# Second attention block of a fused transformer kernel: 21 weight tiles as three one-pass products of float32r halves, gate halves spread among merges, norm squares chunk by chunk

## The chip, the cores and the metric

One core of a Trainium2 chip runs the whole program in one launch. The metric is the device time of one execution, in microseconds. Engines are named as in the profile: PE (TensorE), DVE (VectorE), ACT (ScalarE), POOL (GpSimd), SP (SyncE, which issues most DMAs here).

## The reference, cut to what matters

Two blocks are computed one after the other on a sequence of 512 tokens of width 1024. The first (a gated delta rule beside a forgetting attention, then a SwiGLU feed-forward network, FFN) ends in a norm. The second begins so:

```python
h = modulate(rmsnorm_2(x, norm1_g), shift1, scale1)
q, k, v, cb, cc, cu = split(h @ w_in)             # 512, 128, 128, 512, 512, 512 columns
q, k = rope(rmsnorm_2(q, q_norm_g)), rope(rmsnorm_2(k, k_norm_g))
attn = sliding_window_attention(q, k, v, sinks)   # window 128, 8 query heads, 2 key heads
conv = cb * short_conv(cc * cu, conv_w)           # 3 taps
merged = concatenate([rmsnorm_2(attn), rmsnorm_2(conv)])
x = x + gate1 * (merged @ w_out)
h2 = modulate(rmsnorm_2(x, norm2_g), shift2, scale2)
x = x + gate2 * peer(h2, ...)                     # top-k experts: most of the time, not touched
```

All of it is float32. A result has to agree with a float32 computation.

## The kernel before, in words

Activations lie transposed, 128 features on the partitions and 512 tokens along the row, eight such chunks for 1024 features. A weight tile is 1024 x 128, eight chunks of 128 x 128; one product of it with the activations fills one PSUM bank.

**Order.** Each engine runs its own list of instructions in the order written, and semaphores connect the lists. Nothing is reordered by a planner: an instruction that waits holds up all that stands behind it on its engine.

**The first block.** After the delta rule's preparation a loop goes through `schedule()`: merges of triangular inverses (`merge_p`, `merge_y`; POOL makes their masked operands at L740) alternate with steps of the forgetting attention (`attend_scores`, `attend_turn`, `attend_out`). `gate_half(k, j)` (L1118) is half of a weight tile for the output gate, four tiles in all: tiles 0 and 1 are done inside the preparation, both halves of tile 2 right before the loop, and those of tile 3 after the loop's second `merge_p` and its second `attend_scores`.

**The FFN.** 68 weight tiles (`ITEMS_F`) are each split into a float32r high part by ACT (`split_high`, L1693) and a low part by DVE (`split_low`, L2204), three tiles ahead of PE, and multiplied in three passes (`split_product`, L1201 to L1203: high x high, high x low, low x high). The last eight tiles are the last third of the down projection. Each is added to the residual by DVE (`residual`, L2198).

**The norm between the blocks.** ACT squares each of the eight residual chunks twice (L1749, L1750), once scaled, for two norms. POOL adds the squares up chunk by chunk (`add_square`, L753), and PE turns the sums into means (`mean_sum` L1175, `mean_last` L1180). ACT takes roots (L1731), DVE reciprocals, and DVE and ACT write the modulated input `u2` in halves of 256 tokens (L2326, L1741).

**The second block's input projection.** `first_pair` (L1265) multiplies the first two q tiles while `u2` is still being written. Then 15 tiles go through `product` (L1244), plain float32: q2, q3, k (`for f in range(2, 5)`), and cc0, cu0 to cc3, cu3 and cb0 to cb3 (`conv_products`). For q and k, ACT copies each tile out (L1760), squares it (L1766) and takes the root of a mean (L1756), DVE does a reciprocal (L2363), scales and rotates (L2357 to L2359), and PE makes the mean and the turn (L1250, L1256). DVE uses that loop for the last norm of the residual too: two chunks for each tile (`last_norm`, L2334).

**The window loop.** Eight steps s (four blocks of 128 queries by two key heads). PE: a conv product, four or eight transposes (L1352), scores of the next step (L1333), in steps 1, 3 and 5 a second conv product, then the output (L1367). DVE: mask (L2401), maximum (L2403), in between a part of the convolution (`conv_step`), the copy of the step before (`window_out`, L2378), then the division (L2413). ACT: exponentials (L1797, L1799), copies of the transposes (L1806).

**Behind it.** Norms of both halves of `mix`, `half_mix` (L1385) for the first two output tiles, `product` for the other six, the residual (L2424).

**Transfers.** SP issues them in order, each `fill` after a wait for the reader of what lay in its slot before. Two slots of 16 KB a partition take turns. In the second block SP's list is: F_Q2, F_KV2, two fills F_CU2 (cc and cu), F_CB2 (cb), then a wait for `pool_step` 10 and four DMAs that write zeros to `dense_gates` in HBM (L612, 25.2 MB), then F_OUT2 and F_OUT2 + 1 (output tiles 0 to 3 and 4 to 7), then the next stage's weights. `pool_step` 10 is POOL's memset of the source row (L775), which waits for all eight `last_norm` chunks (`x2_ready`):

```python
pool.wait_ge(S["x2_ready"], DC)
step(pool.memset(zeros, 0.0))
```

Of the kernel before, what the change touches and what calls it, by code (L numbers as in the profile page):

```python
# [21 lines left out]
P = 128  # L22
# [43 lines left out]
CUT, SPLIT_FLOATS = 12675, 22656  # L66
# [53 lines left out]
def program(nc, io):  # L120
    places, n_const = const_places()
    ctx = ExitStack()
    with ctx:
# [11 lines left out]
        with nc.sbuf_tensor("split", [P, SPLIT_FLOATS], F32R) as split:  # L135
            pass
# [134 lines left out]
        keep = top[0]  # L271
        qkr = carve(5, SEC)
        vt2 = carve(SC, P)
        prod = carve(2, SEC + CK2 - 1)
        cc = carve(2, SEC)
        y2 = carve(CW // P, SEC)
        mix = carve(DC, SEC)
        sq2 = carve(2, SEC)
        tm2 = carve(2, SEC)
        ex = carve(PER, 2 * P)  # L280
        pT2 = carve(2, PER * P)
        mxs, nms, rss, ess = (carve(PER) for _ in range(4))
        top[0] = max(top[0], ffn_end)
        cosT, sinT, angT = (carve(SEC) for _ in range(3))
        assert top[0] <= over_rstd - MOD_W
# [30 lines left out]
        gate_of = carve(SEC)  # L316
        zeros = carve(DEN)
# [76 lines left out]

        def chunks_of(i):
# [55 lines left out]
        def tile_out(p):  # L451
# [6 lines left out]
            first = 5 if f == 15 else 0  # L458
# [23 lines left out]
        def _(sp):  # L482
# [126 lines left out]
            fill(F_CB2, halves(F_CB2, w2[:, :, c_cb:c_cb + 512]), "p2_ready", 5 + SC + 2)  # L609
# [5 lines left out]
            for k in range(2):  # L615
                fill(F_OUT2 + k, halves(F_OUT2 + k, wo2[:, :, k * 512:(k + 1) * 512]), "p2_ready", 5 + SC + 4 * (k + 1))
            wq = io["wq"].rearrange("(c p) n -> p c n", p=P)
            for k in range(4):
                reader, count = ("out2_done", 4 * (k + 1)) if k < 2 else ("wq_done", 4 * (k - 1) + 2)
# [210 lines left out]
        def _(pe):  # L830
# [222 lines left out]
            def attend_scores(s):  # L1053
# [4 lines left out]
                else:  # L1058
                    pe.wait_ge(S["proj_taken"], 29)
# [13 lines left out]
            def attend_turn(s):  # L1073

# [33 lines left out]
            def gate_half(k, j):  # L1108
# [6 lines left out]
                elif k == 0:  # L1115
                    pe.wait_ge(S["proj_taken"], FIRST + 1)
                for c in range(DC):
# [14 lines left out]
            for j in range(2):  # L1132
                gate_half(2, j)

            for what, a, s in schedule():
# [1527 lines left out]
```

## Time and profile before

| | us |
|---|---|
| median of three runs | 2430.11 |
| lowest and highest | 2428.63, 2436.08 |
| the profiled execution | 2433.65 |
| its span, first to last instruction | 2431.8 |
| PE's share of the chain that ended last | 95% |

The span is read in stages: projections and merges up to about 490 us, the output projection and the FFN from 490 to 882, the norm to 896, the input projection to 953, the window loop to 1066, the output projection to 1130, query scoring to 1264, and the experts to the end. A row of the timeline gives the start and the duration in us, the engine, the line, out<-in with partitions x elements, and in brackets how long the engine had stood idle and who released it. Matmuls overlap, so that the distance from one start to the next, not the duration, is what one costs.

### The profile page before, as it was taken

To read this page: it belongs to the slowest core of one execution; us is meant where nothing else is said; L and a number is where in the kernel's file an instruction comes from. 1 tells how busy PE (TensorE), PEld (TensorE's weight loads), DVE (VectorE), ACT (ScalarE), POOL (GpSimd) and SP (SyncE) were. 2 spreads that over 40 slices of the span, in tenths; PEclk is the share of its full clock that TensorE was granted. 3 is DMA by queue.
4 is the path that set the end of the run, shared out by engine and by line. 5 is a ranking of instruction groups with operands and counts; after the bars stand their busy time and mean duration, and the time that the engine had idled before them with its cause. 6 is when DMAs were issued, how large, how long until landed. Compare 5 with 4: busy or idle time off the path is not lost.

```text
span 2431.8 us, 33626 instructions
## 1 busy us (share of the span) xinstructions
PE 2394.3 (98%) x11435; PEld 1467.0 (60%) x11435; DVE 1437.0 (59%) x2831; ACT 874.3 (36%) x1385; POOL 1063.3 (44%) x739
## 2 busy tenths in 40 slices
PE   8999999999999989999999999999999999999999
PEld 6888677658888865445554444444444466666665
DVE  4412455456868547444949894222222399989998
ACT  3222223232232242223135555445445433333332
POOL 0001111010000020001788888888888175578886
PEclk9999889999999999999999999999999999999999
DMA  7240100165666312852436666666666799999997
GB/s 206 70 72 1 53 10 10 70 178 162 189 180 196 87 52 70 322 196 87 87 44 149 150 156 151 148 155 154 147 153 155 251 397 382 370 359 374 367 370 286
DMA packets 437700, 426.49 MB, mean 175 GB/s; under 512 B 104808, under 2 KB 359912, under 8 KB 437488
## 3 DMA queue, kind: packets, MB, share of 16 engines
q1 hardware_dynamic: 353456, 332.85, 43.0%
q0 software_dynamic: 84160, 92.58, 15.4%
q8 instruction: 46, 0.75, 0.1%
q14 instruction: 38, 0.31, 0.0%
HBM read 364.28 MB, written 61.05 MB: 175 GB/s over the span
## 4 chain that ended last, share of the span: by engine, by line
PE 95%; DVE 2%; ACT 1%; issue 1%; SPq 0%; POOL 0%; DMA 0%; DVEq 0%; ACTq 0%; POOLq 0%
PE psum L1469 9%; PE psum L1471 9%; PE psum L1470 9%; PE psum L1492 7%; PE psum L1494 7%; PE psum L1493 7%; PE psum L1244 6%; PE psum L889 6%; PE psum L1201 5%; PE psum L1203 5%; PE psum L1202 5%; PE psum L1450 4%; PE psum L1104 1%; PE psum L1081 1%; PE psum L969 1%; PE psum L1062 1%
## 5 line engine op out<-in xcount | busy, mean ns | idle before, releaser
L786 POOL DMA_INDIRECT dense_gates<-arena x384 | 607.2, 1581 | 151.6 <-issue 116.7
L1469 PE MATMUL psum<-arena 128*128 128x512 bf16 x1024 | 389.8, 381 | 0.0
L1471 PE MATMUL psum<-arena 128*128 128x512 bf16 x1024 | 387.6, 379 | 0.0
L1470 PE MATMUL psum<-arena 128*128 128x512 bf16 x1024 | 386.9, 378 | 0.0
L2535 DVE TENSOR_TENSOR arena<-arena,psum 128x1024 bf16<-128x1024 f32 x124 | 151.5, 1222 | 352.1 <-ACT psum L1845 351.5
L1494 PE MATMUL psum<-arena,low 128*128 128x384 bf16 x1024 | 334.3, 326 | 0.0
L1492 PE MATMUL psum<-arena,low 128*128 128x384 bf16 x1024 | 334.3, 326 | 0.0
L1493 PE MATMUL psum<-arena,low 128*128 128x384 bf16 x1024 | 334.3, 326 | 0.0
L1861 ACT ACTIVATE low<-low 128x1024 bf16<-128x1024 f32 x128 | 135.3, 1057 | 294.2 <-PE psum L1494 272.0
L814 POOL DMA_INDIRECT arena<-gelu_spill,arena x128 | 184.8, 1444 | 87.3 <-DMA gelu_spill<-cst 43.3
L806 POOL DMA_INDIRECT arena<-in_v,arena x128 | 178.9, 1398 | 84.0 <-DVE arena L2582 55.9
L1201 PE MATMUL psum<-split 128*128 128x512 f32 x528 | 207.2, 392 | 0.6 <-DVE low L2198 0.6
L1203 PE MATMUL psum<-split 128*128 128x512 f32 x528 | 205.8, 390 | 0.0
L1202 PE MATMUL psum<-split 128*128 128x512 f32 x528 | 205.7, 390 | 0.0
L1851 ACT ACTIVATE cst<-psum 128x512 f32<-128x512 f32 x128 | 76.6, 598 | 307.6 <-PE psum L1471 307.5
L2569 DVE TENSOR_TENSOR low<-low 128x1024 bf16<-128x1024 f32 x128 | 156.9, 1225 | 34.1 <-ACT low L1861 34.1
L1470 PEld LDWEIGHTS psum<-arena 128*128 128x128 bf16 x1024 | 101.2, 99 | 121.4
L1469 PEld LDWEIGHTS psum<-arena 128*128 128x128 bf16 x1024 | 99.6, 97 | 121.3
L1471 PEld LDWEIGHTS psum<-arena 128*128 128x128 bf16 x1024 | 98.9, 97 | 122.6
L2582 DVE SCALAR_TENSOR_TENSOR arena<-arena 128x1024 f32<-128x1024 f32 x127 | 163.2, 1285 | 11.2 <-DMA arena<-in_v,arena 1.2
L753 POOL TENSOR_TENSOR arena<-arena 128x512 f32<-128x512 f32 x25 | 31.6, 1281 | 290.1 <-ACT arena L1784 108.9
L759 POOL DMA_DIRECT2D arena<-in_ada_w x12 | 10.9, 908 | 323.2 <-DVE arena L2231 243.5
(377 smaller groups left out, 3945.2 us busy)
## 6 DMA issues: line engine op xcount, KB each, us to landing
arena<-in_uT SPq DMA_DIRECT2D x128, 512.0 KB, 4.6
low<-in_v SPq DMA_DIRECT2D x128, 512.0 KB, 5.5
gelu_spill<-cst SPq DMA_DIRECT2D x128, 256.0 KB, 3.4
arena<-in_ada_w POOLq DMA_DIRECT2D x12, 2048.0 KB, 9.2
dense_gates<-arena SPq DMA_DIRECT2D x4, 6144.0 KB, 40.0
arena<-gelu_spill SPq DMA_DIRECT2D x128, 192.0 KB, 5.8
arena<-dense_gates SPq DMA_DIRECT2D x128, 192.0 KB, 7.0
low<-in_w_in SPq DMA_DIRECT2D x20, 1024.0 KB, 7.4
```

The source lines that it names most:

```text
L786: pool.indirect_dma_start(gate_cells, bass.IndirectOffsetOnAxis(ap=cell_of[:, n:n + 1], axis=0), gate_of[:, n:n + 1], None, compute_op=ALU ...
L806: pool.indirect_dma_start(vrow[n % ROWS], None, table, bass.IndirectOffsetOnAxis(ap=slot_row[:, n:n + 1], axis=0)).then_inc(S[f"row_in{n % ...
L814: pool.indirect_dma_start(slot_act[:, n:n + 1], None, cells, bass.IndirectOffsetOnAxis(ap=slot_cell[:, n:n + 1], axis=0)).then_inc(S[f"cel ...
L1201: mm(out, wh[:, c, :], hi[:, c, :], start=c == 0, stop=False)
L1202: mm(out, wh[:, c, :], lo[:, c, :], start=False, stop=False)
L1203: last = mm(out, wl[:, c, :], hi[:, c, :], start=False, stop=c == n - 1)
L1469: mm(psum[:, bank, :], hi[:, c, :], h2hi[:, c, :], start=c == 0, stop=False)
L1470: mm(psum[:, bank, :], hi[:, c, :], h2lo[:, c, :], start=False, stop=False)
L1471: last = mm(psum[:, bank, :], lo[:, c, :], h2hi[:, c, :], start=False, stop=c == DC - 1)
L1492: mm(psum[:, f, 0:DEN], vh[:, cols], wh, start=start, stop=False)
L1493: mm(psum[:, f, 0:DEN], vh[:, cols], wl, start=False, stop=False)
L1494: last = mm(psum[:, f, 0:DEN], vl[:, cols], wh, start=False, stop=stop)
```

## The change

21 tiles of the second block (q2, q3, k, all of cc, cu and cb, and output tiles 2 to 7) are split as the FFN's are and multiplied in three passes by a new `product_2`. They go in the order of `ITEMS_2`, through the FFN's three pairs of buffers. ACT writes the high part (`split_high_2`) and DVE the low part (`split_low_2`). The activations `u2`, and later `mix`, get a high and a low part too (`bhi`, `blo`). In the window loop the splits of step s stand in `SPLIT_AT[s]`. The slots' fills now wait for the low parts (`fw_lo`). `last_norm` moves from the q and k loop into the window loop's first four steps. The order of SP's list and the wait for `pool_step` 10 in it stay as they were.

Apart from that, the second half of gate tile 2 moves behind the loop's first `attend_scores`, and the second half of tile 3 behind the first `attend_turn`; and ACT squares each residual chunk when it is ready, among the last FFN tiles, instead of behind them. Tiles are placed anew in the memory to make room.

```diff
+        ITEMS_2 = [("q", 2), ("q", 3), ("k", 0)]
+        ITEMS_2 += [(what, j) for j in range(4) for what in ("cc", "cu")] + [("cb", j) for j in range(4)]
+        ITEMS_2 += [("o", f) for f in range(2, DC)]
+        SPLIT_AT = [(6, 7), (8,), (9, 10), (11,), (12, 13), (14,), (15, 16), (17,)]
...
@@ SP
+                sp.wait_ge(S["fw_lo"], F_ALL + 2 + k)
                 fill(F_CU2 + k, ...
-                     "p2_ready", 4 if k == 0 else 5 + SC)
-            fill(F_CB2, halves(...), "p2_ready", 5 + SC + 2)
+                     "p2_ready", 2 if k == 0 else 5 + SC)
+            fill(F_CB2, halves(...), "fw_lo", F_ALL + place_2["cc", 2])
             sp.wait_ge(S["pool_step"], 10)
             for q in range(4):
                 sp.dma_start(io["dense"]...)
...
-                fill(F_OUT2 + k, halves(...), "p2_ready", 5 + SC + 4 * (k + 1))
+                fill(F_OUT2 + k, halves(...), "fw_lo", F_ALL + place_2[("cb", 0) if k == 0 else ("o", 2)])
...
@@ PE
+            def product_2(bank, i, sig, between=None):
+                pe.wait_ge(S["fw_lo"], F_ALL + i + 1)
+                wh, wl = fwh[i % SPLITS], fwl[i % SPLITS]
                 for c in range(DC):
                     if between and c == 4:
                         between()
+                    mm(psum[:, bank, :], wh[:, c, :], bhi[:, c, :], start=c == 0, stop=False)
+                    mm(psum[:, bank, :], wh[:, c, :], blo[:, c, :], start=False, stop=False)
+                    last = mm(psum[:, bank, :], wl[:, c, :], bhi[:, c, :], start=False, stop=c == DC - 1)
+                last.then_inc(S[sig], 1)
...
-            for j in range(2):
-                gate_half(2, j)
+            gate_half(2, 0)
...
                     attend_scores(s)
-                    if s == 1:
-                        gate_half(3, 1)
+                    if s == 0:
+                        gate_half(2, 1)
...
                         attend_turn(s - 2)
+                    if s == 2:
+                        gate_half(3, 1)
...
@@ ACT
+                if what == "down" and q == 2 and k:
+                    norm_squares(k - 1)
...
+            def split_high_2(i):
+                if i < SPLITS:
+                    act.wait_ge(S["ffn_ps"], F_ALL)
+                else:
+                    sig, count = done_2(i - SPLITS)
+                    act.wait_ge(S[sig], count)
+                n, w = raw_2(i)
+                if i == 0 or raw_2(i - 1)[0] != n:
+                    act.wait_ge(*fill_done(n))
+                f_(fwh[i % SPLITS], w, ACT.Copy).then_inc(S["fw_hi"], 1)
+            for c in range(DC):
+                act.wait_ge(S["shifted"], c + 1)
+                f_(bhi[:, c, :], u2[:, c, :], ACT.Copy).then_inc(S["h2_hi"], 1)
+                if c >= DC - SPLITS:
+                    split_high_2(c - (DC - SPLITS))
...
@@ ACT, window loop
                 ins.then_inc(S["a_tc"], 1)
+                for i in SPLIT_AT[s]:
+                    split_high_2(i)
                 if s == 1:
                     take_c(1)
                 elif s == 6:
                     conv_square(0)
                     conv_square(1)
...
@@ DVE
-                if j < 4:
-                    last_norm(2 * j)
-                    last_norm(2 * j + 1)
+                if j >= 2:
+                    split_low_2(j + 1)
...
@@ DVE, window loop
                     conv_step(s - 1)
                     window_out(s - 1)
+                    for i in SPLIT_AT[s - 1]:
+                        split_low_2(i)
+                if s < 4:
+                    last_norm(2 * s)
+                    last_norm(2 * s + 1)
                 dve.wait_ge(S["a_e"], s + 1)
...
+            for k, c in enumerate((4, 5, 6, 7, 0, 1, 2, 3)):
+                dve.wait_ge(S["h2_hi"], DC + k + 1)
+                dve.tensor_tensor(blo[:, c, :], mix[:, c, :], bhi[:, c, :], ALU.subtract).then_inc(S["h2_split"], 1)
```

## Rows read from the trace of the kernel before

**Rows 1.** Windows: length, busy PE PEld DVE ACT POOL (count), clock, DMA share, GB/s.
```profile
953.00:1066.00 113.00, 112.16 (x328) 53.10 (x327) 49.35 (x91) 29.47 (x96) 1.27 (x1) 1.00 0.74 268
...
1004.00:1008.00 4.00, 4.00 (x10) 1.76 (x10) 3.86 (x7) 1.08 (x5) 0.00 (x0) 1.00 1.06 401
```
**Rows 2.** Groups by line: count, busy us, mean ns, idle before; the page's part 5.
```profile
L1244 PE MATMUL psum<-arena,low 128*128 128x512 f32 x336 | 148.1, 596 | 0.5 <-DVE arena L2342 0.5
L1201 PE MATMUL psum<-split 128*128 128x512 f32 x528 | 207.2, 392 | 0.6 <-DVE low L2198 0.6
```
**Rows 3.** Timeline of PE in the FFN, 57 matmuls in a row.
```profile
699.62 0.39 PE L1201 MATMUL psum<-split 128*128 128x512 f32 x1
...
712.31 0.39 PE L1203 MATMUL psum<-split 128*128 128x512 f32 x1
```
**Rows 4.** Timeline of ACT and DVE in the FFN: splits of one tile and one chunk.
```profile
701.86 1.06 ACT L1693 ACTIVATE split<-low 128x1024 fp32r<-128x1024 f32 x1 [3.30 <-PE psum L1203]
...
708.69 1.22 DVE L2204 TENSOR_TENSOR split<-low,split 128x1024 fp32r<-128x1024 f32 x1
708.81 0.64 ACT L1716 ACTIVATE split<-low 128x512 fp32r<-128x512 f32 x1 [0.44 <-DVE low L2290]
```
**Rows 5.** Timeline from the end of the FFN to the second block's first product.
```profile
873.69 14.88 POOL L753 TENSOR_TENSOR arena<-arena 128x512 f32<-128x512 f32 x12 [101.60 <-ACT arena L1749]
...
881.80 0.69 DVE L2198 TENSOR_TENSOR low<-low,psum 128x512 f32<-128x512 f32 x1 [3.39 <-PE psum L1203]
...
887.40 3.78 PE L1175 MATMUL psum<-arena,cst 128*128 128x512 f32 x4 [5.70 <-POOL arena L753]
...
892.31 0.69 ACT L1731 ACTIVATE arena<-psum,low 128x512 f32<-128x512 f32 x1 [8.54 <-PE psum L1180]
...
896.06 14.05 PE L1265 MATMUL psum<-arena,low 128*128 128x256 f32 x64 [2.93 <-ACT arena L1741]
...
900.36 3.31 ACT L1741 ACTIVATE arena<-arena,low 128x256 f32<-128x256 f32 x8 [1.66 <-DVE arena L2326]
```
**Rows 6.** Windows of 4 us, columns as in Rows 1: after an idle PE.
```profile
886.00:890.00 4.00, 2.60 (x3) 1.13 (x4) 0.00 (x0) 0.00 (x0) 2.57 (x3) 0.50 0.00 0
```
**Rows 7.** Groups by line, 896 to 953 us: the reciprocals of q and k.
```profile
L2363 DVE RECIPROCAL arena<-arena 128x512 f32<-128x512 f32 x5 | 16.8, 3352 | 9.9 <-ACT arena L1756 9.9
```
**Rows 8.** Timeline of step 4 of the window loop: mask, last exponential.
```profile
1003.93 1.23 DVE L2401 TENSOR_TENSOR arena<-psum,cst 128x1024 f32<-128x1024 f32 x1 [1.55 <-PE psum L1333]
...
1008.90 0.19 ACT L1799 ACTIVATE arena<-arena 128x4 f32<-128x4 f32 x1
```
**Rows 9.** Timeline of POOL's memset and SP's queue; then landing of all fills (L499).
```profile
944.13 0.42 POOL L775 MEMSET arena<- 128x384 f32 x1 [55.56 <-DVE low L2334]
...
981.46 50.05 SPq L612 DMA_DIRECT2D dense_gates<-arena  x4
1031.56 31.43 SPq L499 DMA_DIRECT2D low<-in_w_out  x4
...
DMA to landing us min/median/max: 4.9/7.4/28.5
```
**Rows 10.** Timeline of PE, the last step's transposes.
```profile
1061.88 1.04 PE L1352 MATMUL psum<-cst,arena 128*128 128x128 f32 x8
```
**Rows 11.** Timeline of PE among the merges: two gate halves, the fourth merge.
```profile
248.01 7.39 PE L1118 MATMUL psum<-arena,low 128*128 128x264 f32 x32
...
270.30 1.11 PE L971 MATMUL psum<-cst,low 128*128 128x128 f32 x4
```
**Rows 12.** Timeline of PE, four merges of eight matmuls each.
```profile
294.11 1.16 PE L969 MATMUL psum<-arena,low 128*128 128x128 f32 x8
...
300.75 1.16 PE L969 MATMUL psum<-arena,low 128*128 128x128 f32 x8
...
310.76 1.65 PE L969 MATMUL psum<-arena,low 128*128 128x128 f32 x8
...
321.40 2.08 PE L969 MATMUL psum<-arena,low 128*128 128x128 f32 x8
```

More of the change, by code:

```diff
@@ L135, in program @@
         with nc.sbuf_tensor("split", [P, SPLIT_FLOATS], F32R) as split:
+            pass
+        with nc.sbuf_tensor("below", [P, BELOW_2], F32), nc.sbuf_tensor("split_2", [P, 2 * DC * SEC], F32R) as split_2:
             pass
@@ L271, in program @@
         keep = top[0]
+        sq2 = carve(2, SEC)
+        tm2 = carve(2, SEC)
+        pT2 = carve(2, PER * P)
+        assert top[0] == CUT + BELOW_2
+        bhi, blo = (split_2[:, k * DC * SEC:(k + 1) * DC * SEC].rearrange("p (c t) -> p c t", c=DC) for k in range(2))
+        top[0] += 2 * DC * SEC
+        mxs, nms, rss, ess = (carve(PER) for _ in range(4))
+        assert top[0] <= ffn_end - 2 * SPLITS * DC * P
+        top[0] = ffn_end
+        cosT, sinT, angT = (carve(SEC) for _ in range(3))
+        assert top[0] <= over_rstd - MOD_W
+        vt2 = angT.rearrange("p (a b) -> p a b", a=SC)
+        ex = carve(PER, 2 * P)
+        mix = carve(DC, SEC)
+        y2 = carve(CW // P, SEC)
+        over_zeros = arena_floats - (DC * SEC + P + SEC + DEN)
+        assert top[0] <= over_zeros
+        top[0] = over_zeros + DEN
         qkr = carve(5, SEC)
-        vt2 = carve(SC, P)
         prod = carve(2, SEC + CK2 - 1)
         cc = carve(2, SEC)
[L276 to L285, printed above, removed]
         top[0] = over_rstd + 2 * TP
@@ L1393, in _ @@
             for f in range(2, DC):
-                if f == 4:
-                    pe.wait_ge(*fill_done(F_OUT2 + 1))
+                if f == 2:
+                    pe.wait_ge(S["h2_split"], 2 * DC)
                 pe.wait_ge(S["res2_done"], f - 1)
-                product(f % 2, slot_cols(F_OUT2 + f // 4), slice(f % 4 * P, (f % 4 + 1) * P), mix, "out2_done")
+                product_2(f % 2, place_2["o", f], "out2_done")
             mean_sum(u2, 4 * SUMS + 1)
@@ L1666, in _ @@
                     take(ORDER.index(12 + m // 2))
-            take(ORDER.index(14))
             for what, a, s in schedule():
@@ L1722, in _ @@
                     split_high(ahead)
-            def squares2(ready):
-                for c in range(DC):
-                    act.wait_ge(S[ready], c + 1)
-                    f_(u2[:, c, :], xT2[:, c, :], ACT.Square).then_inc(S["sq_ready"], 1)
+                if what == "down" and q == 2 and k:
+                    norm_squares(k - 1)
             def std2(ready, bank, row, bias):
@@ L1742, in shift @@
                            ).then_inc(S["shifted" if j else "half_shifted"], 1)
-            f_(rstd[:, 1, 0:1], eps[:, 0:1], ACT.Sqrt)
-            act.wait_ge(S["col_sq"], 2)
-            act.wait_ge(S["mod_acc"], MODS * P // MOD_W + 1)
-            for c in range(DC):
-                act.wait_ge(S["res_done"], 3 * DC + c + 1)
-                f_(u2[:, c, :], xT2[:, c, :], ACT.Square, scale=col_sq[:, c:c + 1]).then_inc(S["sq_ready"], 1)
-                f_(sq1[:, c, :], xT2[:, c, :], ACT.Square).then_inc(S["sq1_ready"], 1)
+            norm_squares(DC - 1)
             std2(3, 6, 0, eps_sq)
@@ L1822, in _ @@
                     mix_root(3 - c)
-            act.wait_ge(S["m_done"], DC)
-            squares2("res2_done")
+            for c in (4, 5, 6, 7, 0, 1, 2, 3):
+                act.wait_ge(S["m_done"], (c + 4) % DC + 1)
+                f_(bhi[:, c, :], mix[:, c, :], ACT.Copy).then_inc(S["h2_hi"], 1)
+            for c in range(DC):
+                act.wait_ge(S["res2_done"], c + 1)
+                f_(u2[:, c, :], xT2[:, c, :], ACT.Square).then_inc(S["sq_ready"], 1)
+                if 2 <= c < 5:
+                    split_high_2(place_2["o", c + 3])
             std2(5, 6, 0, eps)
@@ L2329, in _, with split_low_2 @@
             modulated(0, col_n1, DC)
+            def split_low_2(i):
+                dve.wait_ge(S["fw_hi"], F_ALL + i + 1)
+                dve.tensor_tensor(fwl[i % SPLITS], raw_2(i)[1], fwh[i % SPLITS], ALU.subtract).then_inc(S["fw_lo"], 1)
+            for c in range(DC):
+                dve.wait_ge(S["h2_hi"], c + 1)
+                dve.tensor_tensor(blo[:, c, :], u2[:, c, :], bhi[:, c, :], ALU.subtract).then_inc(S["h2_split"], 1)
+                if c >= DC - SPLITS:
+                    split_low_2(c - (DC - SPLITS))
             dve.wait_ge(S["std_ready"], 5)
@@ L2416, in _ @@
             window_out(SC * KV - 1)
+            for i in SPLIT_AT[SC * KV - 1]:
+                split_low_2(i)
             for g in (1, 0):
```

75 lines of the change are left out of this document (48 added, 27 removed).

## The prediction

> **What bounds the kernel now.** The chain of work that ended last lies on PE for 95%. That tells which engine is late on average, not what an edit is worth, so I went through the stages that the change touches and asked in each which wait ends last. In the window loop PE is busy for 112.16 of 113 us [rows 1] and idles 0.5 us ahead of all its products [rows 2]: PE bounds it, and DVE and ACT have more than half of the time free. Behind the FFN, by the timeline, PE stands and waits for POOL's sums. And in the timeline of SP's queue 25.2 MB of zeros are written during the window loop; nobody waits for them now (their rows are named where they are priced). That queue is what I think decides this change, so keep it in mind while PE's gain is worked out.
>
> **PE's gain for one tile.** Two records stand for one float32 matmul: 336 of them take 148.1 us, 0.441 us each with the start of every product in it, some 0.429 inside one; the 16 of a tile are 6.87 us [rows 2]. In the FFN 57 one-pass matmuls start within 12.69 us, one per 0.2266 us [rows 3], so 24 of them take 5.44 us. One tile saves 1.43 us, 21 tiles 30 us, if PE is what each of them waits for.
>
> The Trainium skill (FP8 and Floating Point Precision, TensorE Precision Notes) says that true float32 takes four passes through the array. By that rule three passes save a quarter, 1.72 us per tile; the rows show less, since a split pass costs 0.2266 us and a quarter of a float32 matmul 0.2145. For the six tiles that reach the end in my sum the rule would give 10.3 us, the rows 8.6, which I take.
>
> **The splits.** A tile costs ACT 1.06 and DVE 1.22 us, a chunk of activations 0.64 on ACT [rows 4] and 0.69 on DVE, as another DVE pass of 512 columns [rows 5]. That is 22 and 26 us for the tiles, 10 and 11 us for twice eight chunks.
>
> **Norm squares: 7.9 us earlier.** Now POOL starts at 873.69 and needs 14.88 us for twelve adds, 1.24 each; PE waits 5.70 us for them and starts at 887.40 [rows 5]. With squares made as each residual comes (one per 18 x 0.2266 = 4.08 us) the two adds of a chunk, 2.5 us, are done before the next; those of chunk 6, whose residual starts at 881.80 - 4.08 = 877.7, end near 881.6. The last chunk goes to PE directly: residual until 882.5, square 883.2, mean 884.3. The root moves from 892.31 [rows 5] to 884.4, and the gap in which the clock fell to 0.50, the 1.2 GHz level [rows 6], closes. ACT has 1.3 us more for each tile of 4.08, POOL's adds can delay a low part by one add; three tiles of lead cover both.
>
> **Input projection: 8.2 us earlier.** The first pair, 896.06 to 910.1 [rows 5], goes from 888.2 to 902.2. ACT's list now has eight chunk copies (0.57 each back to back) and three splits ahead of its first copy of a q tile; behind the shifts, which end at 903.7 [rows 5] less 7.9, that lasts until 903.4. The first mean, which waits for copy and square, comes at 904.8, not 902.2. DVE ends its low parts at 905.3, does the reciprocal of the second norm (3.35, as [rows 7]) and only at 908.8 the first of q. From there each tile costs DVE a reciprocal of 3.35 [rows 7], one pass to scale, three to rotate and a split: 7.3 us, against PE's 5.44 and two matmuls of 0.86. PE no longer bounds it; it stalls 1.0 us at the first turn, 0.4 at the last, 1.6 before the first scores. Those come at 945.1 instead of 953.2: of 7.9 + 4 x 1.43 us the stage keeps 8.2.
>
> **The window loop, up to step 3.** A wide step needs 5.2 us from the mask to the last exponential [rows 8]; DVE's own part (two passes of 1.23 and three tiny ones) is 2.95, half as wide (steps 0 and 1) 1.9. Behind it DVE now does, by the widths, a part of the convolution (2.1), `window_out` (0.7), one or two splits (1.23 each), two `last_norm` chunks (1.4) and the division (1.6, narrow 1.1). Step 1: 1.9 + 2.1 + 0.7 + 2.45 + 1.4 + 1.1 = 9.7 us, while PE has one output and one product, 6.5: the transposes come at 963.1 and PE has stood 3.5 us. Step 2, behind a second product and `gated`: 3.0 + 2.1 + 0.7 + 1.2 + 1.4 + 1.6 = 10 us against 5.44; transposes at 982.5, 4.4 us lost. In step 3 the last two `last_norm` chunks end at **993.0**. This is the point that counts. Before, they ended at 944.1, and POOL's memset followed [rows 9], in time for a queue that came to its wait at 981.
>
> **The transfer wall.** SP's order is unchanged: zeros behind `pool_step` 10, F_OUT2 behind the zeros. Before, the zeros were issued from 981.46, and issuing them held SP for 50.05 us; F_OUT2 was issued at 1031.56 and landed 28.5 us later, at 1060.1, though the median fill needs 7.4: it lay behind the zeros [rows 9]. (28.5 is the largest landing of that line; I take it for this fill, the only one issued behind zeros.) Nobody minded, as its first reader, `half_mix`, stands behind step 7. From 981.46 to 1060.1 went 29.4 MB (2.1 of F_CB2, issued just before, 25.2 of zeros, 2.1 of F_OUT2), 374 GB/s. Now the memset ends at 993.5 and the zeros start near 993.8; F_CB2 landed long before; 27.3 MB at 374 GB/s are 73 us, with 1.5 us to start: F_OUT2 lands at **1068.3**. But its reader has moved forward: `split_high_2(15)` in ACT's step 6, which PE's work alone would let run near 1042. Behind that wait on ACT are split 16, two squares, and all exponentials of step 7; DVE needs both high parts before it divides step 7; PE needs DVE. PE ends its last conv product near 1049 and stands for 26 us. From the landing on: two splits 2.1, two squares 1.2, exponentials 2.2, division 1.6, with waits 7.35 us: the transposes of step 7 start at 1075.6, before at 1061.88 [rows 10]. Here the change is 13.8 us behind, and all that PE saved since step 3 is gone.
>
> **Behind the wall.** After 5.7 idle us PE worked at a clock of 0.50 [rows 5, 6]; after 26 it will too: transposes, conv mean and part of the last output at half rate cost 2.2 us (0 if the clock stays). The eight low parts of `mix`, 5.5 us, end 0.4 us later than the first residual lets PE go on. Then six tiles gain 8.6 us. Sum: 13.8 + 2.2 + 0.4 - 8.6 = 7.8 us slower. SP's next weights, for the query stage, start no later than now.
>
> **Gate halves: 1 us more, and the clock.** A half is 3.6 us of PE [rows 11]. The loop's first merge starts that much earlier, but `merge_p` 2 now finds its operand not ready (POOL makes it from DVE's merge 0, which stands behind the scores of step 1): PE idles some 2.7 us where a half had covered it, and the half comes later, ahead of the scores of step 3. By this order the fourth merge moves from 270.30 [rows 11] to 271.2. Bounds: 3.6 us won if a half goes wholly into idle time, 2.7 lost. Worth more is the clock: in this loop eight matmuls that take 1.16 us at times take 2.08, and then two merges with two attention steps between them are 10.64 us apart instead of 6.64 [rows 12]. 16 us in that state cost 6. Moving PE's work by some us can take such an episode away or add one; the trace doesn't say which.
>
> **The sum.** 2433.65 of the profiled execution (span 2431.8 and 1.85 around it) plus 7.8 plus 1.0 is 2442.4. That execution is 3.5 us above the median of the runs; against the median it is 2430.1 + 8.8 = **2439 us**.
>
> **Rivals.**
> *The zeros don't hold F_OUT2 up* (0.16). Then step 7's transposes follow PE's and DVE's own work at 1050.4, 11.5 us earlier than before; one more split ahead of the last squares costs 0.8: 11.5 - 0.8 - 0.4 + 8.6 - 1.0 = 17.9 us won, 2412. Against it stands the landing of 28.5 us. The Trainium skill (DMA: Bandwidth & Descriptors, Issuing engines are not separate DMA queues) says that DMAs from SP, ACT and POOL run on the same engines and interleave; if a fill interleaved so with zeros of its own queue, this rival would be right, and no row here shows that.
> *Full gain* (0.04): DVE keeps up everywhere, 30 + 7.9 us: 2392. DVE's sums above speak against it.
> *Faster zeros* (0.13): at 400 GB/s, as around 1004 [rows 1], F_OUT2 lands 4.7 us earlier: 2434.
> *A clock episode less* (0.18): 2433. *One more* (0.13): 2445. This is the slower side's own mechanism: it decides where PE's idle pieces before 271 us fall close together.
> *The forecast* (0.36): 2439, own range 2433 to 2444.
>
> **Chances and range.** A measurement of this kernel can tell 0.3%, 7.3 us: from 2422.8 to 2437.4 is no change. Faster: 0.16 + 0.04, and 0.04 from two favourable cases together: 0.24. Same: the rest of these two cases and the forecast's low end: 0.33. Slower: 0.43. The range 2412 to 2448 leaves out the full gain, half of the first rival and the bad cases added up, 0.16.
>
> **What would show it.** In the profile after: product matmuls 0.227 us apart; the root behind the FFN at 884.4; the memset at 993 and zeros issued right behind it; a hole of 20 to 30 us in PE between 1049 and 1076, where ACT's first split of an output tile waits for a DMA; a clock of 0.50 behind it; DVE's reciprocals of q and k nearly back to back. Without the hole the first rival is right. If the memset comes before 980, my chain of DVE in steps 1 to 3 is too long; if the hole is there and the time still under 2423, the wall is right and its neighbours are mis-sized.

## The result and the profile after

The changed kernel takes 2447.66 us (median of 20 runs, 2436.09 to 2452.09) against 2432.01 us for the kernel before, taken beside it (20 runs): a ratio of 1.0066 with a 95% interval of 1.0056 to 1.0077. It is slower by 0.66%. The profiled execution took 2449.53 us, span 2447.7, against 2433.65 and 2431.8 before. Differences below are between these two executions, unless another run is named.

Line numbers have moved: the fill is L531 (L499 before), the zeros L645 (L612), the memset L810 (L775), the last transposes L1389 (L1352), half_mix L1422 (L1385), and the new products are L1287 to L1289.

The page of the changed kernel, line of the chain's engines in part 4; SP's queue stands in it, with DMA behind it, where the kernel before had PE for 95%:

```profile
PE 90%; DVE 4%; SPq 3%; ACT 1%; DMA 1%; issue 0%; POOL 0%; DVEq 0%; ACTq 0%; POOLq 0%
```

The chain of waits of the changed kernel, 1030 to 1100 us, in order of time (start, us, what; lines of bare issue time are left out). It is the prediction's wall in one piece: zeros, the fill issued behind them, its landing, ACT's split of the first output tile, squares, exponentials, division, transposes.

```profile
1029.40 16.16 SPq L645
...
1045.61 17.49 SPq L531
...
1063.14 12.77 DMA low<-in_w_out
...
1075.99 1.12 ACT split L1802 x2
...
1077.93 1.13 ACT arena L1842 x2
1079.06 1.97 ACT arena L1855 x8
...
1081.57 1.24 DVE arena L2494
...
1082.85 1.97 PE psum L1389 x8
```

The same places in the timelines (POOL, SP, ACT, PE), with the idle time before each in brackets:

```profile
999.06 0.42 POOL L810 MEMSET arena<- 128x384 f32 x1 [116.17 <-DVE low L2411]
...
999.50 46.06 SPq L645 DMA_DIRECT2D dense_gates<-arena  x4
1045.61 23.69 SPq L531 DMA_DIRECT2D low<-in_w_out  x4
...
1075.99 2.03 ACT L1802 ACTIVATE split<-low 128x1024 fp32r<-128x1024 f32 x2 [28.45 <-DMA low<-in_w_out]
...
1082.85 1.97 PE L1389 MATMUL psum<-cst,arena 128*128 128x128 f32 x8 [26.96 <-DVE arena L2494]
```

Before, the memset stood at 944.13 and the zeros at 981.46 [rows 9], and the transposes at 1061.88 [rows 10]. Now the memset comes 55 us later, since it waits for last_norm (DVE L2411), the zeros 18 us later, and PE stands 26.96 us ahead of the transposes.

Windows of 4 us in the window loop (columns as in [rows 1]), which the prediction did not foresee: PE stands in the first and the fourth, and in the ones behind each the clock is between 0.61 and 0.50, the 1.2 GHz level.

```profile
960.00:964.00 4.00, 1.34 (x8) 0.92 (x8) 2.73 (x6) 0.45 (x1) 0.00 (x0) 1.00 0.87 287
964.00:968.00 4.00, 4.00 (x11) 2.75 (x10) 0.00 (x0) 1.11 (x2) 0.00 (x0) 0.53 0.64 238
968.00:972.00 4.00, 4.00 (x13) 3.15 (x12) 0.00 (x0) 0.00 (x0) 0.00 (x0) 0.61 0.00 0
980.00:984.00 4.00, 1.47 (x7) 0.89 (x5) 3.90 (x7) 0.73 (x5) 0.00 (x0) 1.00 0.00 0
984.00:988.00 4.00, 2.60 (x10) 2.17 (x11) 1.31 (x2) 0.59 (x2) 0.00 (x0) 0.59 0.02 4
988.00:992.00 4.00, 4.00 (x10) 2.26 (x9) 0.81 (x1) 2.40 (x4) 0.00 (x0) 0.50 0.00 0
```

Where the time went, from starts in the timelines of both executions:

| point | before | after | difference | forecast for it |
|---|---|---|---|---|
| FFN's end (first fill of the block) | 871.36 | 872.48 | +1.1 | +1.0 |
| root behind the FFN | 892.31 | 885.59 | -6.7 | -7.9 +1.0 |
| first scores | 953.24 | 945.18 | -8.1 | -8.2 +1.0 |
| transposes of step 1 | 970.88 | 962.86 | -8.0 | 963.1 after |
| transposes of step 2 | 989.10 | 985.40 | -3.7 | 982.5 after |
| zeros issued | 981.46 | 999.50 | +18.0 | 993.8 after |
| output tiles landed (both halves) | 1062.8 | 1075.9 | +13.1 | 1068.3 after |
| transposes of step 7 | 1061.88 | 1082.85 | +21.0 | +13.8 +1.0 |
| half_mix | 1073.34 | 1096.04 | +22.7 | |
| mean behind the output | 1128.35 | 1144.23 | +15.9 | +8.8 |
| span | 2431.8 | 2447.7 | +15.9 | +8.8 |

A fill is two DMAs, one for each half. The prediction took the landing of the first half, 1060.1, for that of the whole fill. In the kernel before, the view of the fill's line for 1031 to 1050 us has both halves: the second was issued at 1048.4 and landed 14.4 us later, at 1062.8.

```profile
L499 SPq DMA_DIRECT2D low<-in_w_out x2: 2129/9480/16830, 1031.6 to 1048.4; - x2
...
DMA to landing us min/median/max: 14.4/21.5/28.5
```

### The profile page after: what moved, and what is told of

Read it like the earlier page. It is cut to its first block, busy times and chain, and to the rows that moved or that the text cites. A ratio compares the mean times of both kernels' runs of the same rounds, so it can differ in the third digit from the quotient of the medians.

```text
span 2447.7 us, 34059 instructions
## 1 busy us (share of the span) xinstructions
PE 2377.3 (97%) x11603; PEld 1503.7 (61%) x11603; DVE 1470.0 (60%) x2868; ACT 903.5 (37%) x1422; POOL 1047.3 (43%) x739
## 4 chain that ended last, share of the span: by engine, by line
PE 90%; DVE 4%; SPq 3%; ACT 1%; DMA 1%; issue 0%; POOL 0%; DVEq 0%; ACTq 0%; POOLq 0%
PE psum L1506 9%; PE psum L1507 9%; PE psum L1508 9%; PE psum L1531 7%; PE psum L1530 7%; PE psum L1529 7%; PE psum L924 6%; PE psum L1241 5%; PE psum L1242 5%; PE psum L1243 5%; PE psum L1487 4%; SPq L645 2%; PE psum L1141 1%; PE psum L1118 1%; PE psum L1004 1%; PE psum L1097 1%
## 5 line engine op out<-in xcount | busy, mean ns | idle before, releaser
L849 POOL DMA_INDIRECT arena<-gelu_spill,arena x128 | 177.5, 1387 | 87.1 <-DMA gelu_spill<-cst 43.3
L841 POOL DMA_INDIRECT arena<-in_v,arena x128 | 167.8, 1311 | 102.6 <-DVE arena L2670 78.1
L1728 ACT ACTIVATE split<-low 128x1024 fp32r<-128x1024 f32 (+1 forms) x68 | 70.3, 1035 | 199.2 <-PE psum L1243 199.2
```

The costliest lines, as they stand in the source:

```text
L841: pool.indirect_dma_start(vrow[n % ROWS], None, table, bass.IndirectOffsetOnAxis(ap=slot_row[:, n:n + 1], axis=0)).then_inc(S[f"row_in{n % ...
L849: pool.indirect_dma_start(slot_act[:, n:n + 1], None, cells, bass.IndirectOffsetOnAxis(ap=slot_cell[:, n:n + 1], axis=0)).then_inc(S[f"cel ...
```

## The experiments

The theory: the late last_norm holds the memset, the memset the zeros, the zeros the fill that is issued behind them, and the fill holds ACT. e1 cuts the first link, e2, e3, e11 and e4 cut the third, and e8 and e5 put last_norm elsewhere. The rivals were that the hole belongs to DVE's and ACT's longer lists, and that a fill overtakes the zeros. All ratios are against the kernel before, run beside each.

| run | median us | ratio, 95% interval |
|---|---|---|
| changed kernel | 2447.66 | 1.0066 [1.0056, 1.0077] |
| e1 early memset | 2424.30 | 0.9963 [0.9942, 0.9984] |
| e2 first fill ahead | 2441.24 | 1.0038 [1.0020, 1.0056] |
| e3 both fills ahead | 2424.37 | 0.9970 [0.9951, 0.9990] |
| e4 fill from ACT | 2443.40 | 1.0040 [1.0022, 1.0058] |
| e11 last quarter behind | 2431.20 | 1.0005 [0.9993, 1.0017] |
| e8 last_norm back | 2416.99 | 0.9940 [0.9923, 0.9957] |
| e5 last_norm spread | 2418.47 | 0.9945 [0.9926, 0.9964] |
| e6 norm squares alone | 2426.24 | 0.9975 [0.9962, 0.9989] |
| e7 gate halves alone | 2433.42 | 0.9999 [0.9982, 1.0016] |
| e9 e8 + low part behind | 2413.44 | 0.9930 [0.9908, 0.9951] |
| e10 e5 + low part behind | 2407.55 | 0.9908 [0.9890, 0.9927] |
| e12 e10 + last quarter behind | 2408.99 | 0.9913 [0.9893, 0.9933] |

**The memset alone (e1).**

```diff
-            pool.wait_ge(S["x2_ready"], DC)
+            pool.wait_ge(S["std_ready"], 5)
             step(pool.memset(zeros, 0.0))
```

> The changed kernel, with one edit: POOL's memset of the zeros row waits for the roots behind the FFN instead of for all eight last_norm chunks. DVE's list and SP's order stay. Theory (the transfer wall: the late last_norm holds the zeros, the zeros hold the fill of the output tiles, the fill holds ACT): zeros are issued near 960 instead of 999.5, F_OUT2 lands near 1035 instead of 1075.9, ACT's splits 15 and 16 run at once near 1047.5, PE's hole before the last transposes shrinks from 27 to about 1 us, transposes at 1056 instead of 1082.9; with the two clock drops behind the hole gone as well (about 3 us) 2418 us, 2412 to 2424. Rival (the hole belongs to DVE's and ACT's longer lists, the DMA is only the last of several waits): transposes stay later than 1070, 2435 or more. Rival (the zeros, now beside the conv weights, delay something earlier): a new wait for a fill in steps 1 to 4.

Measured: 2424.30 us. Its timelines of SP and PE:

```profile
958.29 50.11 SPq L645 DMA_DIRECT2D dense_gates<-arena  x4
1008.45 32.33 SPq L531 DMA_DIRECT2D low<-in_w_out  x4
...
1055.21 1.09 PE L1389 MATMUL psum<-cst,arena 128*128 128x128 f32 x8 [1.32 <-DVE arena L2494]
```

The zeros go out at 958.29, the stand ahead of the last transposes is 1.32 us, and the transposes come at 1055.21. DVE's and ACT's lists are the same as in the changed kernel: the hole isn't theirs. One wait on POOL, which had stood idle for 116 us, makes 25 us of difference by the ratios (1.0066 and 0.9963). The profiled execution took 2419.16, near the expected 2418; the median of 2424.30 lies just above the expected 2412 to 2424.

**Order in the queue (e2, e3).** In both, `fill(F_OUT2, ...)` goes ahead of the wait and the zeros; in e3 `fill(F_OUT2 + 1, ...)` does too:

```diff
+            fill(F_OUT2, ...)
+            fill(F_OUT2 + 1, ...)        # e3; in e2 behind the zeros
             sp.wait_ge(S["pool_step"], 10)
             for q in range(4):
                 sp.dma_start(io["dense"]...)
```

> The changed kernel, but SP issues the first fill of output tiles (F_OUT2) ahead of its wait for the memset and ahead of the zeros; the second (F_OUT2 + 1) stays behind them. Theory: the low part it waits for is written near 997.7, so the fill lands near 1004 and costs the zeros about nothing; splits 15 and 16 don't wait and the last transposes come at 1056. But split 17, in ACT's list of step 7, is the first of the second fill, which still lands behind the zeros, near 1078 (29.4 MB from 998 at 364 GB/s); ACT's squares, and with them the norms of mix, stand behind that split. From split 17 to half_mix are 10.2 us: half_mix at 1088 instead of 1096: 2440 us, 2436 to 2444. The wall moves by one step, not away. Rival (only the first fill is waited for on time; split 17 hides behind the last output): half_mix near 1070, 2420.

> The changed kernel with SP's order turned: both fills of output tiles ahead of the zeros. Theory: the first fill lands near 1004, the second, whose slot comes free with the last conv tile's low part near 1040.6, near 1047; no split waits for a DMA; transposes of step 7 near 1056, half_mix near 1068 instead of 1096; the zeros go out from 1041 to about 1115, and nobody waits for them before the gates. 2419 us, 2413 to 2425, about as with the early zeros. Rival (the query weights, now behind the zeros in the queue, become the wall): they land near 1118, and the query products wait: 2425 to 2435.

Measured for e2: 2441.24. In PE's timeline the transposes of step 7 are free, and the hole stands a step later, ahead of the conv means (L1360) that wait for ACT's squares; ACT's waits (us in total, times, longest) name the cause:

```profile
1060.40 1.09 PE L1390 MATMUL psum<-cst,arena 128*128 128x128 f32 x8 [1.34 <-DVE arena L2495]
...
1079.48 4.11 PE L1360 MATMUL psum<-arena,cst 128*128 128x512 f32 x4 [14.89 <-ACT arena L1843]
...
1088.63 13.97 PE L1423 MATMUL psum<-arena,low 128*128 128x512 f32 x32 [0.52 <-DVE arena L2505]
```

```profile
ACT split L1803 <- DMA low<-in_w_out: 15.2, 1, 15.2
```

half_mix at 1088.63 was expected at 1088. The split's tile is the third product behind half_mix; it holds the squares up only because it stands ahead of them on ACT.

Measured for e3: 2424.37. No split waits for a DMA. But the zeros now lie ahead of the next stage's loads, and the rival named for this run is there as well, in PE's timeline at the query stage, with the sub-keys rather than the query weights:

```profile
1127.57 10.57 PE L1448 MATMUL psum<-arena,low 128*128 128x256 f32 x40 [8.34 <-DMA arena<-in_subk]
```

In the early-zeros kernel PE stood 3.79 us there, so 4.5 us of e3's gain went into the new wait.

**A dose (e11).** The last of the four DMAs of zeros goes out behind both fills; nothing else is changed.

```diff
-            for q in range(4):
+            for q in range(3):
                 sp.dma_start(io["dense"]...)
...
             for k in range(2):
                 fill(F_OUT2 + k, ...)
+            for q in range(3, 4):
+                sp.dma_start(io["dense"]...)
```

> The changed kernel, but the last quarter of the zeros (6.3 MB) goes out behind both fills of output tiles. A dose: theory (what is in the queue ahead of the fill sets its landing, by bytes): 6.3 MB at 374 GB/s are 16.8 us, so F_OUT2 lands near 1059 instead of 1075.9, the last transposes come near 1066 instead of 1082.9, the hole is 10 us instead of 27: 2431 us, 2427 to 2434. Rival (a fill waits for the whole run of zeros, or for SP's issue alone): below 2425 or above 2440.

Measured: 2431.20. In its profiled execution all is about 7 us later from the FFN on (first fill of the block at 879.54), so distances count, not times:

```profile
1006.55 29.85 SPq L645 DMA_DIRECT2D dense_gates<-arena  x3
1036.45 22.88 SPq L531 DMA_DIRECT2D low<-in_w_out  x4
1059.37 3.13 SPq L651 DMA_DIRECT2D dense_gates<-arena  x1
...
1072.83 1.97 PE L1392 MATMUL psum<-cst,arena 128*128 128x128 f32 x8 [5.19 <-DVE arena L2497]
```

By the chain of waits of e11 the fill landed at 1065.9, 59.3 us behind the first zeros; in the changed kernel 76.4. The difference of 17.1 us for 6.3 MB was expected to be 16.8. PE's stand is 5.19 and not 10, since PE came later itself: behind its stand of 2.06 us in step 5 the clock fell to 0.50 here, and from these transposes to the next it took 20.86 us, where the changed kernel, with the same stand and the full clock, took 16.09. So the bytes ahead in SP's queue set the landing. Most of it goes through the issue: SP came to the fill 29.9 us behind the first zeros, in the changed kernel 46.1.

**Another queue (e4).** The two DMAs of the first fill are issued by ACT in step 4, while SP's zeros run.

```diff
+                if s == 4:
+                    act.wait_ge(S["fw_lo"], F_ALL + place_2["cb", 0])
+                    for c in (0, 4):
+                        act.dma_start(slot_cols(F_OUT2, 512)[:, c:c + 4, :], ...)
```

> The changed kernel, but the first fill of output tiles is issued by ACT, in step 4 (near 1011), while SP's zeros are under way; the second fill stays on SP behind the zeros. What is asked: does a fill from another engine's queue overtake the zeros? If the queues share the 16 engines about evenly, 2.1 MB land within 12 to 15 us, near 1025, splits 15 and 16 don't wait, and the next wait is split 17's for the second fill near 1078, as with the first fill ahead: 2440 us. If the engines work the zeros off first, the fill lands near 1070 as now: hole as before, 2446 to 2448. The first is the rival of the prediction (zeros don't hold the fill up), for two queues; for one queue the changed kernel has answered it.

Measured: 2443.40, between the two forecasts. ACT's timeline, and the landing of its two DMAs (us from issue to landing, view of the line):

```profile
1017.43 1.83 ACTq L1870 DMA_DIRECT2D low<-in_w_out  x2
...
DMA to landing us min/median/max: 11.9/14.0/16.0
```

2.1 MB landed within 16.0 us while the zeros ran on; the fill behind the zeros in SP's own queue took 30 us from its first issue to its landing in the changed kernel (1045.61 to 1075.9), after SP had been held for 46 us by issuing the zeros. So another engine's queue does overtake. The Trainium skill (DMA: Bandwidth & Descriptors, Issuing engines are not separate DMA queues) says that DMAs of different issuers run on the same engines and interleave; this run agrees, with landings 11.9 and 16.0 us behind the issue. What it doesn't give is a fill passing others in its own queue, and that was my first rival. The time hardly moved because split 17, whose fill stayed on SP, then waited for 21.2 us, as in e2.

**last_norm (e8, e5).** e8 puts last_norm back to where it stood before, two chunks for each of four tiles of the q and k loop. e5 keeps e1's memset and puts the pairs into steps 0, 3, 4 and 6.

```diff
+                if j < 4:                     # q and k loop, e8
+                    last_norm(2 * j)
+                    last_norm(2 * j + 1)
...
-                if s < 4:                     # window loop, e8 and e5
-                    last_norm(2 * s)
-                    last_norm(2 * s + 1)
+                if s in (0, 3, 4, 6):         # e5
+                    k = (0, 3, 4, 6).index(s)
+                    last_norm(2 * k)
+                    last_norm(2 * k + 1)
```

> The changed kernel with last_norm back in the q and k loop, where it stood before; POOL's memset waits for it as ever. Theory: the memset comes near 940 and the zeros start behind the last conv fill near 960, so that the hole goes as with the early zeros; DVE, which bounds the q and k loop, has 1.4 us more for each of four tiles: first scores some 4 to 5.6 us later (near 950); the stands of steps 1 and 2 shrink by 1.4 each, with 0 to 6 us of clock. 2418 to 2427 us, against 2424 of the early zeros and 2447 of the changed kernel. Rival (the hole doesn't hang on where last_norm stands): 2447 or more.

> The kernel with the early zeros, and last_norm's pairs of chunks in steps 0, 3, 4 and 6 of the window loop instead of 0 to 3. There PE stood 2.66 and 3.94 us ahead of the transposes of steps 1 and 2, for DVE's division, and in the trace its clock stood at 0.50 for some us behind each. Theory (DVE's list is the bound of these two steps, and the clock falls for these stands): steps 1 and 2 have 1.4 us less in front of the division, so the stands are 1.26 and 2.5 us; 2.8 us for sure, and up to 6 more if the clock then holds; steps 3, 4 and 6, where PE doesn't stand, have room. 2415 to 2421 us against 2424 of the early zeros. Rival (the stands come from ACT's exponentials or the splits alone): stands as before, 2424.

Measured: 2416.99, a little under the expected range, and 2418.47, inside it; the intervals of e5 and e1 overlap. e8's memset comes at 935.08 and its zeros go out at 960.41. From the first pair to the first scores it took 58.64 us against 55.84 in the changed kernel: last_norm costs the q and k loop 2.8 us. (The changed kernel's first pair ran 1.6 us longer at a lower clock, but the mean behind it, which waits for ACT, comes 15.84 us after the pair's start there and 15.85 in e8.) That buys back the whole hole. In e5, PE's stands ahead of the transposes of steps 1 and 2 (2.66 and 3.94 us in e1) are each 1.3 us shorter, as two chunks of last_norm take 1.4:

```profile
961.18 0.66 PE L1389 MATMUL psum<-cst,arena 128*128 128x128 f32 x4 [1.33 <-DVE arena L2495]
...
979.20 1.09 PE L1389 MATMUL psum<-cst,arena 128*128 128x128 f32 x8 [2.62 <-DVE arena L2495]
```

```profile
964.00:968.00 4.00, 4.00 (x19) 3.28 (x18) 0.00 (x0) 0.00 (x0) 0.00 (x0) 1.00 1.03 342
```

So DVE's list is what PE stands for. Behind the shorter stand e5's window of 964 to 968 us has the full clock, where the changed kernel had 0.53. The shorter stand alone doesn't bring that: e8 has the same stand of 1.33 us in step 1, and its window is at 0.50.

```profile
961.63 0.66 PE L1389 MATMUL psum<-cst,arena 128*128 128x128 f32 x4 [1.33 <-DVE arena L2494]
```

```profile
964.00:968.00 4.00, 4.00 (x10) 2.75 (x9) 0.00 (x0) 0.00 (x0) 0.00 (x0) 0.50 1.00 326
```

**The two small parts (e6, e7).** Each put alone into the kernel before.

```diff
+                if what == "down" and q == 2 and k:
+                    norm_squares(k - 1)                 # e6
...
-            for j in range(2):
-                gate_half(2, j)
+            gate_half(2, 0)                             # e7, and so on as in the change
```

> The kernel before with one part of the change alone: norm squares chunk by chunk. Theory: the root behind the FFN comes 7.8 us earlier as in the changed kernel (892.3 to 884.5), the first pair takes up to 1.6 us longer since the clock drop then lies on it (15.66 against 14.05 us), and behind it PE bounds the projection, the window loop and all to the query stage, so that 6.2 to 7.8 us reach the end: 2425 us against 2432. Rival (given back later, to a fill that lands no earlier): less than 3 us.

> The kernel before with one part alone: the moved gate halves. Theory: 1.0 us slower by PE's order (between 2.7 won and 3.6 lost), and what the clock's episodes in the merge loop add or take, up to 6 us either way: 2433 us, 2426 to 2440. In the changed kernel's one profiled execution the FFN ended 1.1 us later, and episodes of the lower clock between 240 and 370 us were there in both. Rival (the idle pieces that the halves filled now let the clock fall once more in most executions): 2438 or more.

Measured: 2426.24 and 2433.42, beside 2433.5 of before. The norm squares bring 7.3 us by the medians and 6.1 by the ratio (2.7 to 9.2 by the interval), the gate halves nothing that can be told: the interval reaches from 4.4 us won to 3.9 lost.

**The second low part behind the division (e9, e10), and e11's order with it (e12).** In steps in which DVE writes two low parts, the second goes behind the softmax's division: e9 does this to e8, e10 to e5. e12 adds e11's order to e10.

```diff
-                    for i in SPLIT_AT[s - 1]:
-                        split_low_2(i)
+                    split_low_2(SPLIT_AT[s - 1][0])
...
                                   ALU.mult).then_inc(S["a_p"], 1)
+                if s and len(SPLIT_AT[s - 1]) > 1:
+                    split_low_2(SPLIT_AT[s - 1][1])
```

> The kernel with last_norm back in the q and k loop, and in the steps in which DVE writes two low parts (1, 3, 5, 7) the second one moved behind the division of the softmax; zeros early by last_norm's place. Theory (DVE's list ahead of the division is what PE stands for, in steps 1, 5 and 7 with 1.33, 2.07 and 1.32 us, and the tile is wanted only a product later): these stands shrink by 1.2 us each, 3.7 in sum, and the clock drops that follow them, 1 to 4 us, can go: 2410 to 2414 us against 2417. Rival (the low part, now later, holds up the next product or the next step's mask): no gain, 2417.

> The same edit on the kernel with early zeros and last_norm in steps 0, 3, 4 and 6: there PE stood 1.33, 2.06 and 1.32 us in steps 1, 5 and 7. Theory: as with the other, 3.7 us and up to 4 us of clock: 2411 to 2415 us against 2418.5. That both gain alike would show that the place of last_norm no longer matters once the zeros don't hang on it.

> The fastest version so far (early zeros, last_norm in steps 0, 3, 4 and 6, second low part behind the division) with the last quarter of the zeros behind both fills of output tiles as well. In its profile, now that all else is earlier, the wall is met again: ACT's split of the first output tile waits 6.7 us for its DMA, PE stands 5.24 us ahead of the last transposes, and the clock falls to 0.50 behind that. Theory: with 6.3 MB less ahead of it the fill lands 16.8 us earlier, that wait goes, PE stands about 1 us, as in the sister kernel: 4 us, and up to 3 of clock: 2400 to 2404 us against 2407.5. Rival (the query weights, behind the last quarter, are late, or another wait stands right behind this one): 2406 to 2408.

Measured: 2413.44, 2407.55 and 2408.99. e9 can't be told from e8, whose interval reaches from 0.9923 to 0.9957. e10 is 0.92% faster than the kernel before and 1.6% faster than the changed one. It did better than expected although the wall is met again in it, since all else is now earlier; in e12 that stand is gone, and nothing is won. The last transposes of e10, then of e12:

```profile
1037.97 1.97 PE L1389 MATMUL psum<-cst,arena 128*128 128x128 f32 x8 [5.24 <-DVE arena L2494]
```

```profile
1039.62 1.09 PE L1392 MATMUL psum<-cst,arena 128*128 128x128 f32 x8 [0.20 <-DVE arena L2497]
```

e12 was expected at 2400 to 2404 us and missed that. In its profiled execution the transposes of step 1 already come 2.4 us later than in e10's (952.32 against 949.90), and behind those of step 2 the clock is at 0.50 where e10 kept 1.00, which makes it 14.97 us to the next ones instead of 10.71; half_mix starts at 1051.79 and 1051.01. Why the two differ there before the edit can act isn't settled; the times of e10 and e12 can't be told apart.

## Why the prediction was right in its mechanism, and which step failed

The direction, the place and the mechanism held: slower, by the wall that was named, with the hole from 1055.9 to 1082.85 us (forecast 20 to 30 us long, between 1049 and 1076). The size didn't: 2447.66 against 2439, 0.3 us inside the range, and 15.9 us in the profiled executions against 8.8. That the range held is luck: its upper end was room for one more clock episode in the merge loop (2445), and the time was lost in the window loop. The step that failed is the price of PE's stands in the window loop up to step 3; a smaller miss is a misread landing in the transfer wall. By the steps of the prediction:

- **One tile.** Three products of output tiles in a row start at 1117.03, 1122.47 and 1127.91, 5.44 us apart as said; the six tiles gain 8.1 us up to the mean, where 8.6 was said. Right.
- **Norm squares.** The root is 7.8 us earlier against the FFN's end (20.95 us before, 13.11 after). Right. The gap of 5.70 us closed, but not the clock's drop: PE still stood 2.93 us for the modulation, as before, now the clock was lower in the first pair (0.65 from 888 to 892 us), and that took 15.66 us instead of 14.05. It cost nothing here, since ACT's list ends no earlier: in e8 the pair took 14.05 and PE then stood 1.80 us for ACT.
- **Input projection.** First scores at 945.18, forecast 945.1; the transposes of step 1 at 962.86, forecast 963.1. Right.
- **The window loop, up to step 3: the step that failed.** The stands were forecast as 3.5 and 4.4 us and were 2.66 and 3.93. But behind both the clock fell, and the prediction, which priced that behind the big hole, put it at nothing here without giving a reason. Behind the first stand the scores took 2.93 us and the product 7.87 (966.38 to 974.25), two steps later, at the full clock, 1.92 and 5.71 (1001.62 to 1009.25). Behind the second, transposes and scores took 5.61 us (985.40 to 991.01), a step later at the full clock 2.94. DVE's mask, which starts the chain to the last `last_norm` chunk, waits for these scores. So the transposes of step 2 came 2.9 us late, the zeros 5.7 us late (999.50, not 993.8). The prediction's rows had both cases: a drop behind a stand of 5.70 us [rows 5, 6], and a first pair of 14.05 us behind one of 2.93 [rows 5], with the clock at 1.00 from 896 to 908 us.

PE, then DVE, in the changed kernel:

```profile
963.45 3.01 PE L1370 MATMUL psum<-arena 64*128 64x256 f32 x8
966.38 0.80 PE L1287 MATMUL psum<-split 128*128 128x512 f32 x1
...
974.25 1.07 PE L1404 MATMUL psum<-arena 128*64 128x512 f32 x2
...
985.40 1.97 PE L1389 MATMUL psum<-cst,arena 128*128 128x128 f32 x8 [3.93 <-DVE arena L2494]
987.30 3.78 PE L1370 MATMUL psum<-arena 64*128 64x256 f32 x8
991.01 3.67 PE L1404 MATMUL psum<-arena 128*64 128x512 f32 x4
...
991.19 1.22 DVE L2477 TENSOR_TENSOR arena<-psum,cst 128x1024 f32<-128x1024 f32 x1 [5.84 <-PE psum L1370]
```

- **The transfer wall.** 27.3 MB went in 76.4 us where 74.5 was said: 1.9 us more. The queue was not slower than before: the 374 GB/s came from the first half's landing. To the landing of the whole fill at 1062.8, 29.4 MB took 81.3 us, 361 GB/s, and by that rate the same sum gives 77.1 us. From the landing to the transposes 6.9 us, forecast 7.35.
- **Behind the wall.** To half_mix 1.7 us more than before (2.2 said), but half_mix itself ran into a second drop (15.67 us instead of 13.97), so 1.3 more up to the next product where 0.4 was said.
- **Gate halves.** +1.0 said, +1.1 in the one profiled execution, nothing in 12 runs of the part alone. Clock episodes in the merge loop are there in every profiled execution, and they move single executions by more than the 6 us that were said: with the same first block, the first fill comes at 860.78 us in e9 and at 879.54 in e11. The medians of e7 and of the kernel before differ by 0.08 us, so for a median the weight given to episodes was too large.

Together: 5.7 + 1.9 - 0.4 - 1.0 (the gate's, already in the start of the zeros) = 6.2 ahead of the transposes, and 0.9 behind them (-5.1 instead of -6.0): 7.1 us, the miss of the sum.

The rivals: that zeros don't hold the fill up is refuted (e1, e2, e11), for a fill in the same queue. Faster zeros: from the first zeros to the landing of both halves it was 357 GB/s, before 361, so no faster. "Full gain" was called unlikely because of DVE, and e8 to e10 bear that out: without the wall PE still stands for DVE in four steps of e8's window loop, and e10, with early zeros and shorter lists ahead of the division, gains 24 of the 38 us.

No run took the stands away and left the zeros late, but pairs of executions with the same stands and the same work on DVE in these steps tell what a drop costs. From the transposes of step 1 to those of step 2 e5 takes 18.02 us at the full clock and e8 21.20 with the drop: 3.2 us. From the transposes of step 2 to the end of the scores behind them e10 takes 2.94 us at 1.00 and e12 5.61 at 0.50: 2.7 us. Together that is 5.9 us, and the zeros were 5.7 late.

What stays open: why the clock falls behind a stand in one execution and not in another. In the six profiled executions with the changed kernel's stands of 2.7 and 3.9 us (it, e1 to e4 and e11) it fell behind both.

## What to carry to other kernels

When a step is moved to where its engine has time, list who waits for it on every queue: here an idle engine's memset hung on it, and on the memset a 25 MB transfer that nobody had waited for, until another part of the change brought forward the reader of the fill behind it. Price a stand of PE not only by its length but also by the slower matmuls that can follow it. When a transfer is made of several DMAs, read the landing of the last one. And a DMA that is wanted soon goes ahead of the bulk one in its queue, or into another engine's queue, as soon as its slot is free; then look what comes behind the bulk one, as the sub-keys did in e3.

## What was not expected of the hardware

A stand of PE is sometimes followed by the lower clock and sometimes not, at the same length. Behind 1.33 us in step 1 e5 kept 1.00 and e8 fell to 0.50, as shown above. Behind 2.06 us in step 5 the changed kernel kept 1.00 and e11 fell. Behind 2.6 us in step 2 e10 kept 1.00, while e9 and e12 fell: their eight transposes take 1.97 us instead of 1.09. In each of these comparisons PE and DVE have the same work in that step.

Step 5 in the changed kernel, then in e11:

```profile
1029.29 1.09 PE L1389 MATMUL psum<-cst,arena 128*128 128x128 f32 x8 [2.06 <-DVE arena L2494]
```

```profile
1036.30 1.97 PE L1392 MATMUL psum<-cst,arena 128*128 128x128 f32 x8 [2.06 <-DVE arena L2497]
```

Step 2 in e10 with the window behind it, then in e9 and in e12:

```profile
967.91 1.09 PE L1389 MATMUL psum<-cst,arena 128*128 128x128 f32 x8 [2.61 <-DVE arena L2494]
```

```profile
968.00:972.00 4.00, 4.00 (x19) 2.64 (x20) 0.97 (x1) 2.96 (x4) 0.00 (x0) 1.00 1.06 402
```

```profile
969.54 1.97 PE L1389 MATMUL psum<-cst,arena 128*128 128x128 f32 x8 [2.58 <-DVE arena L2493]
```

```profile
970.36 1.97 PE L1392 MATMUL psum<-cst,arena 128*128 128x128 f32 x8 [2.61 <-DVE arena L2497]
```
